# PEER routing decode: candidates laid out in two parts, low ranks compared with 20 of them and high ranks with all 50

## The chip, the cores and the metric

The kernel runs on one core of a Trainium2 chip. The metric is device time in microseconds (us), from the start to the end of one execution. Three runs of the kernel before took 1103.86, 1105.05 and 1106.35 us, median 1105.05. Its parts are TensorE (PE in the profile; PEld is its weight load), VectorE (DVE), ScalarE (ACT), GpSimd (POOL) and SyncE (SP, which issues most DMAs).

## The reference, cut to what matters

One decoder layer over 256 tokens of width 1024: three groups of attention heads with one output projection and a layer norm, then PEER, and a second layer norm. The change lies in PEER. For each token and each of 8 heads:

```python
v1, i1 = lax.top_k(s1, 16)           # of 128 sub-keys, first half
v2, i2 = lax.top_k(s2, 16)           # second half
cand     = v1[..., :, None] + v2[..., None, :]          # 16 x 16
cand_idx = i1[..., :, None] * 128 + i2[..., None, :]
top_s, top_j = lax.top_k(cand, 16)
experts = take_along_axis(cand_idx, top_j)
gate = softmax(top_s)
```

The output is the sum over the 128 (head, rank) slots of gate x gelu(x . u[expert]) x v[expert], with 16384 experts. All is float32.

## The kernel before, in words

**Candidates.** Both lists are sorted, so the pair (i, j) (from 0) can be among the best n only if (i + 1)(j + 1) <= n. For n = 16 these are 50 pairs of 256. `COUNT[i] = 16 // (i + 1)` says how many j a row i has, and rows with equal counts are written together: `RUNS` has 7 entries.

**Tiles.** The 256 tokens are T = 2 tiles of 128, one token in a partition. The expert stage runs over NK = 128 blocks of 128 experts, dense: `expert_in(c)` on TensorE is 24 matmuls for block c (8 pieces of the contraction, three products of split-precision halves), then ScalarE takes the gelu, and `expert_out(c)` multiplies with v. A block needs its u weights split: ScalarE copies the high half (`u_split`, line 948, ring of three), VectorE subtracts it from the weights for the low half (`fill`, line 1319). TensorE waits for that low half before each block.

**Order on VectorE** (in-order; the list is written out by hand). Subkey tops of tile 0 (`subkey_tops`, `top16`, lines 1322 to 1341), `route(0, False)`, `fill(3)`, eight times a pair of subkey tops of tile 1 with one fill, `route(1, True)`, the softmax denominators (lines 1408 to 1415), fills up to N0 - 1, then 64 gate groups, each with a fill. With `mixed` true, `route` and `top16` put a fill behind nearly each step: one after the candidates, three in `top16`, twelve in the comparison. The fills so far are counted at compile time: NROUTE = 27 at the end of `route(1, True)`.

**`route(t, mixed)`** (line 1347). It turns the indices to floats (1348), multiplies the first half's by 128 (1354), adds up values and indices of the candidates for each run (1359), takes the top 16 of the 50 of each head (1364), hands out the shifted values (1365), and then finds the expert number of each rank. That is a comparison with all candidate positions: for two heads at a time an is_equal of 2 x 16 ranks x 50 positions (1373), a multiply by the candidates' expert numbers (1378) and a reduce over the 50 (1382). Four such groups cover the 8 heads, in `eq`, 6400 columns of the arena. Lines 1386 to 1392 split the expert number into block and row, three `tensor_scalar` and one `scalar_tensor_tensor`, each waiting for the one before.

**Around it.** TensorE, in the meantime, computes the queries and subkey scores of tile 1; the last of 32 copies of them is ScalarE's line 960 (`q_saved`). Then come the expert blocks. The transposes of the routes stand ahead of block NTURN = 28, and from block N0 = 32 on each of 64 blocks is preceded by the gate matmuls of four tokens. Blocks below N0 put their gelu into the arena directly; blocks from N0 on go through the buffer `gel`, with a multiply for each on VectorE (1450). The arena columns of those later blocks must be set to one beforehand. GpSimd does most of it:

```python
pool.wait_ge(q_saved, 4 * PH)
pool.wait_ge(x1_split, 4)
nc.gpsimd.memset(arena[:, N0 * S:A_S1], 1.0)                         # 401
nc.gpsimd.memset(arena[:, A_END:A_V], 1.0).then_inc(ones_low, 1)     # 402
```

A third (404) waits for the shifted values of both tiles, and three more (418 to 420) stand behind the first one-hots of the gate stage. A_END is the end of `eq`.

Of the kernel before, what the change touches and what calls it, by code (L numbers as in the profile page):

```python
# [10 lines left out]
ALU = mybir.AluOpType  # L11
ACT = mybir.ActivationFunctionType
AX_X = mybir.AxisListType.X

P = 128
# [12 lines left out]
PH = 8  # L28
NK = 128
TK = 16  # L30
# [3 lines left out]
TAKEN = -3e38  # L34
TWO_PI = (6.28125, 0.0019350051879882812, 2 * np.pi - 6.28125 - 0.0019350051879882812)
PI_IN = 3.1415925
N0 = 32
NROUTE = 27
NTURN = 28
POOL_HOT = 2  # L40
GN = S // 4
UR, UH = 6, 3
# [16 lines left out]
SLOTS = 16  # L59


COUNT = [TK // (i + 1) for i in range(TK)]
OFF = [sum(COUNT[:i]) for i in range(TK)]
NCAND = sum(COUNT)
RUNS = []
for _i in range(TK):
    if RUNS and RUNS[-1][2] == COUNT[_i]:
        RUNS[-1] = (RUNS[-1][0], RUNS[-1][1] + 1, COUNT[_i])
    else:
        RUNS.append((_i, 1, COUNT[_i]))  # L70

K_ID, K_IOTA, K_TRI, K_CB, K_FREQ = 0, 128, 256, 512, 512 + T * NC
# [36 lines left out]
A_EX = A_S1 + 2048  # L111
A_R = A_EX + 1024
A_EQ = A_R + 1472
A_END = A_EQ + PH * TK * NCAND
A_XT0 = A_WMQ
A_V = A_ALL - 1024

# [11 lines left out]
def peer_layer_kernel(nc, x, xT, memT, positions, w_tok, w_memq, w_memk, w_memv, w1k, w1v, w2k, w2v, peT,  # L129
                      w_out, ln1, wq, subk, uT, pv, ln2, consts, out):  # L130
    with ExitStack() as ctx:
# [23 lines left out]
        kc = slab[:, 6144:6144 + K_ALL]  # L155
# [8 lines left out]
        def ar(at, n):  # L164
            return arena[:, at:at + n]

        ident = kc[:, K_ID:K_ID + P]
        iota = kc[:, K_IOTA:K_IOTA + P]


# [36 lines left out]
        h = ar(A_H, T * C_ALL).rearrange("p (t n) -> p t n", t=T)  # L207
# [34 lines left out]
        IF = ar(A_R, 256).rearrange("p (b k) -> p b k", b=2 * PH)  # L242
        cand = ar(A_R + 256, PH * NCAND).rearrange("p (h c) -> p h c", h=PH)
        cande = ar(A_R + 656, PH * NCAND).rearrange("p (h c) -> p h c", h=PH)
        tv = ar(A_R + 1056, 128).rearrange("p (h k) -> p h k", h=PH)
        ti = ar(A_R + 1184, 128).bitcast(U32).rearrange("p (h k) -> p h k", h=PH)
        tf = ar(A_R + 1312, 128).rearrange("p (h k) -> p h k", h=PH)
        gs = ar(A_R + 1440, 16)
        ex = ar(A_EX, 768).rearrange("p (t a s) -> p t a s", t=T, a=3)
        te = ar(A_EX + 768, 256).rearrange("p (t h k) -> p t h k", t=T, h=PH)  # L250
        eq = ar(A_EQ, PH * TK * NCAND)
        assert A_END <= A_WMQ
        G = arena[:, :].rearrange("p (c t) -> p c t", c=NK)
        ln2_sb = ar(0, 2048).rearrange("p (a n) -> p a n", a=2)
# [135 lines left out]
        def _(pool):  # L390
# [9 lines left out]
            pool.wait_ge(x1_split, 4)  # L400
            nc.gpsimd.memset(arena[:, N0 * S:A_S1], 1.0)
            nc.gpsimd.memset(arena[:, A_END:A_V], 1.0).then_inc(ones_low, 1)
            pool.wait_ge(g_shift, 2)
# [15 lines left out]
            nc.gpsimd.memset(arena[:, A_V:A_ALL], 1.0)  # L419
            nc.gpsimd.memset(arena[:, A_R + 4096:A_END], 1.0).then_inc(ones_high, 1)  # L420
            for g in range(2, GN):
# [7 lines left out]
        def _(pe):  # L429
# [317 lines left out]
            def turn_routes():  # L747
                for t in range(T):
                    pe.wait_ge(route_ready, t + 1)
                    for a in range(3):  # L750
                        last = nc.tensor.transpose(ps[:, 2 + t, a * P:(a + 1) * P], ex[:, t, a, :], ident)
                    last.then_inc(pe_rT, 1)

            def gates(g):
                pe.wait_ge(oh_ready, g + 1)
                pe.wait_ge(oh2_ready, g + 1)
                pe.wait_ge(oh3_ready, g + 1)
                if g >= GB:
                    pe.wait_ge(pre_gated, g - GB + 1)
                for q in range(4):  # L760
                    last = mm(ps[:, gate_bank(g), q * P:(q + 1) * P], hot(g)[:, 0, q, :], hot(g)[:, 1, q, :],
                              q == 0, True)
                last.then_inc(pe_g, 1)

            pe.wait_ge(x1_split, 4)
            for c in range(NK):
                if c == NTURN:
                    turn_routes()
                if 0 <= c - N0 < GN:
                    gates(c - N0)  # L770
                expert_in(c)
# [29 lines left out]
        def _(act):  # L801
# [142 lines left out]
            def u_split(c):  # L944
                act.wait_ge(u_in[c % UR], (c // UR + 1) * 16)
                if c >= UH:
                    act.wait_ge(pe_h, c - UH + 1)
                nc.scalar.copy(hi[:, c % UH, :], u_raw(c)).then_inc(u_hi, 1)  # L948
# [17 lines left out]
            def gelu(c):  # L966
                act.wait_ge(pe_h, c + 1)
                if c < N0:
                    nc.scalar.activation(arena[:, c * S:(c + 1) * S], ps[:, c % 2, 0:S], ACT.Gelu).then_inc(gelu_done, 1)
                else:  # L970
                    if c >= N0 + 2:
                        act.wait_ge(gated, c - N0 - 1)
                    nc.scalar.activation(gel[:, c % 2, :], ps[:, c % 2, 0:S], ACT.Gelu).then_inc(gelu_done, 1)  # L973
# [28 lines left out]
            for c in range(NK):  # L1002
                gelu(c)
                if c + UH < NK:
                    u_split(c + UH)
                if c + UH == NROUTE - 1:
                    route_exp()
                if c == NTURN - 1:
                    save_routes()
                    act.wait_ge(rT_saved, T)  # L1010
                    onehot(0)
                    fill_ones(0)
                if c == NTURN:
                    fill_ones(1)
# [21 lines left out]
        def _(dve):  # L1036
            v = nc.vector
            count = [0]

            def did(ins):  # L1040
                count[0] += 1
                ins.then_inc(dve_chain, 1)

            def settle():
                dve.wait_ge(dve_chain, count[0])
# [297 lines left out]
            def spread(mixed, n=1):  # L1343
                if mixed:
                    fill(n)

            def route(t, mixed):
                did(v.tensor_copy(IF, IX[:, t, :, :]))
                settle()
                i1 = IF.rearrange("p (h a) k -> p h a k", a=2)[:, :, 0, :]  # L1350
                i2 = IF.rearrange("p (h a) k -> p h a k", a=2)[:, :, 1, :]
                v1 = V[:, t, :, :].rearrange("p (h a) k -> p h a k", a=2)[:, :, 0, :]
                v2 = V[:, t, :, :].rearrange("p (h a) k -> p h a k", a=2)[:, :, 1, :]
                did(v.tensor_scalar(i1, i1, float(NK), None, ALU.mult))
                settle()
                for r0, r, c in RUNS:
                    sl = slice(OFF[r0], OFF[r0] + r * c)
                    for o, a1, a2 in ((cand, v1, v2), (cande, i1, i2)):
                        did(v.tensor_tensor(o[:, :, sl].rearrange("p h (r c) -> p h r c", r=r),  # L1359
                                            a1[:, :, r0:r0 + r].unsqueeze(3).to_broadcast([P, PH, r, c]),  # L1360
                                            a2[:, :, 0:c].unsqueeze(2).to_broadcast([P, PH, r, c]), ALU.add))
                spread(mixed)
                settle()
                top16([(tv[:, hh, :], ti[:, hh, :], cand[:, hh, :]) for hh in range(PH)], mixed)
                v.tensor_tensor(te[:, t], tv, tv[:, :, 0:1].to_broadcast([P, PH, TK]), ALU.subtract).then_inc(g_shift, 1)

                did(v.tensor_copy(tf, ti))
                settle()
                for h0 in range(0, PH, 2):
                    eqh = eq[:, h0 * TK * NCAND:(h0 + 2) * TK * NCAND].rearrange("p (h k c) -> p h k c", h=2, k=TK)  # L1370
                    eqm = eqh.rearrange("p h k c -> p (h k) c")
                    tfl = tf[:, h0:h0 + 2, :].rearrange("p h k -> p (h k)")
                    did(v.tensor_tensor(eqm, tfl.unsqueeze(2).to_broadcast([P, 2 * TK, NCAND]),  # L1373
                                        kc[:, K_IOTA:K_IOTA + NCAND].unsqueeze(1).to_broadcast([P, 2 * TK, NCAND]),
                                        ALU.is_equal))
                    spread(mixed)
                    settle()
                    did(v.tensor_tensor(eqh, eqh, cande[:, h0:h0 + 2, :].unsqueeze(2).to_broadcast([P, 2, TK, NCAND]),  # L1378
                                        ALU.mult))
                    spread(mixed)  # L1380
                    settle()
                    did(v.tensor_reduce(tfl, eqm, AX_X, ALU.add))  # L1382
                    spread(mixed)
                settle()
                tfl = tf.rearrange("p h k -> p (h k)")
                did(v.tensor_scalar(ex[:, t, 0, :], tfl, 1.0 / NK, -(NK - 1) / (2.0 * NK), ALU.mult, ALU.add))
                settle()
                did(v.tensor_scalar(ex[:, t, 0, :], ex[:, t, 0, :], MAGIC, None, ALU.add))
                settle()
                did(v.tensor_scalar(ex[:, t, 0, :], ex[:, t, 0, :], -MAGIC, None, ALU.add))  # L1390
                settle()
                did(v.scalar_tensor_tensor(out=ex[:, t, 1, :], in0=ex[:, t, 0, :], scalar=-float(NK), in1=tfl,
                                           op0=ALU.mult, op1=ALU.add))
                settle()
# [56 lines left out]

            assert filled[0] == NROUTE
            while filled[0] < N0 - 1:
# [109 lines left out]
```

## Time and profile before

| | us |
|---|---|
| median of 3 runs | 1105.05 |
| profiled execution, device time | 1104.46 |
| its span, first to last instruction | 1102.6 |
| TensorE busy | 1045.7 (95%) |
| VectorE busy | 772.2 (70%) |
| ScalarE busy | 433.0 (39%) |
| GpSimd busy | 109.0 (10%) |
| chain that ended last: TensorE / VectorE | 83% / 14% of the span |
| TensorE waiting for VectorE's low halves (line 1319) | 18.6, the longest 12.0 |

The page divides the span by engine; the chain of waits follows the work back from the last instruction, at each step to what released it. The mean granted TensorE clock was 0.964 of full speed. A stretch in which an engine stands in the chain is one where its work sets the end; its busy share elsewhere says little.

### The profile page before, as it was taken

The numbers are of one execution on the slowest core, as the hardware profiler recorded it, in microseconds if no ns is written. First come the engines' busy times: TensorE is split into PE (matmuls) and PEld (weight loads), VectorE is DVE, ScalarE is ACT, GpSimd is POOL, SyncE is SP. The second block draws the span as 40 slices with busy tenths as digits, with TensorE's granted clock in tenths as the row PEclk, the third lists the DMA queues.
The fourth block names the chain that finished last, engine by engine and source line by source line (L and its number), as shares of the span: only waits on it lengthen the run. The fifth ranks groups of instructions, "written<-read, shape, count | busy, mean of one in ns | idle before, by whom it ended". The sixth has DMA issues, their size and how long they took to land.

```text
span 1102.6 us, 17393 instructions
## 1 busy us (share of the span) xinstructions
PE 1045.7 (95%) x6508; PEld 912.4 (83%) x6508; DVE 772.2 (70%) x1817; ACT 433.0 (39%) x767; POOL 109.0 (10%) x210
## 2 busy tenths in 40 slices
PE   6999889899598999999999999989999999999996
PEld 2458766489588999999999999988888888888885
DVE  1253345368999969999999975556666666666667
ACT  0242233322333464554554544443333333333341
POOL 1000000000300043333333300000000000000000
PEclk9989659999899999999999999999999999999999
DMA  9607100059244554444444445546555555555551
GB/s 336 284 1 286 39 1 0 1 172 341 80 135 143 183 170 138 136 147 140 134 147 142 135 159 185 183 180 239 197 195 191 191 193 192 197 196 195 192 191 38
DMA packets 48610, 176.50 MB, mean 160 GB/s; under 512 B 5120, under 2 KB 6160, under 8 KB 47248
## 3 DMA queue, kind: packets, MB, share of 16 engines
q1 hardware_dynamic: 48128, 173.82, 45.9%
q0 software_dynamic: 400, 1.58, 0.4%
q8 instruction: 52, 0.85, 0.3%
q14 instruction: 30, 0.25, 0.1%
HBM read 174.33 MB, written 1.05 MB: 159 GB/s over the span
## 4 chain that ended last, share of the span: by engine, by line
PE 83%; DVE 14%; DMA 1%; ACT 1%; issue 1%; SPq 0%; DVEq 0%
PE ps L431 81%; DVE lo L1319 2%; DVE arena L1328 1%; DVE arena L1378 1%; DVE arena L1382 1%; DVE arena L1373 1%; DMA arena<-in_w_tok 1%; PE ps L579 1%; DVE arena L1325 1%; DVE arena L1334 1%; DVE hi L1319 0%; DVE ahl L1319 0%; DVE arena L1359 0%; ACT arena L874 0%; PE ps L490 0%
## 5 line engine op out<-in xcount | busy, mean ns | idle before, releaser
L431 PE MATMUL ps<-x1hl,hi 128*128 128x256 f32 x2216 | 380.3, 286 | 18.6 <-DVE lo L1319 17.2
L431 PEld LDWEIGHTS ps<-x1hl,hi 128*128 128x128 f32 x2216 | 328.1, 192 | 20.8 <-issue 12.2
L431 PE MATMUL ps<-hi,ahl 128*128 128x512 f32 x992 | 266.6, 390 | 3.0 <-DVE lo L1473 3.0
L431 PEld LDWEIGHTS ps<-hi,ahl 128*128 128x128 f32 x992 | 186.8, 188 | 42.0 <-issue 3.1
L1024 ACT CAST hi<-slab 128x1024 fp32r<-128x1024 f32 x128 | 134.5, 1053 | 206.9 <-PE ps L431 206.9
L431 PE MATMUL ps<-x1hl,lo 128*128 128x256 f32 x688 | 195.0, 283 | 0.0
L1473 DVE TENSOR_TENSOR lo<-slab,hi 128x1024 fp32r<-128x1024 f32 x128 | 155.9, 1218 | 0.0
L431 PE MATMUL ps<-lo,ahl 128*128 128x512 f32 x496 | 153.3, 390 | 0.0
L431 PEld LDWEIGHTS ps<-x1hl,lo 128*128 128x128 f32 x688 | 132.2, 192 | 0.0
L431 PE MATMUL ps<-arena 128*128 128x128 f32 (+5 forms) x800 | 114.4, 304 | 4.8 <-ACT arena L874 3.6
L431 PEld LDWEIGHTS ps<-arena 128*128 128x128 f32 (+2 forms) x800 | 101.8, 202 | 19.9 <-issue 9.5
L1319 DVE TENSOR_TENSOR lo<-slab,hi 128x1024 fp32r<-128x1024 f32 x86 | 106.0, 1234 | 16.9 <-ACT hi L948 16.6
L431 PE MATMUL ps<-arena,slab 128*128 128x512 f32 (+2 forms) x256 | 105.3, 565 | 10.7 <-DMA arena<-in_w_tok 9.7
L948 ACT CAST hi<-slab 128x1024 fp32r<-128x1024 f32 x107 | 111.2, 1040 | 0.4 <-DMA slab<-in_uT 0.4
L431 PEld LDWEIGHTS ps<-lo,ahl 128*128 128x128 f32 x496 | 93.6, 189 | 19.5
L1485 DVE CAST ahl<-arena 128x256 fp32r<-128x256 f32 x124 | 36.4, 294 | 103.6 <-PE ps L431 103.5
L973 ACT ACTIVATE gel<-ps 128x256 f32<-128x256 f32 x96 | 36.9, 384 | 163.8 <-PE ps L431 163.8
L431 PEld LDWEIGHTS ps<-arena,slab 128*128 128x128 f32 x256 | 48.9, 224 | 53.3 <-issue 39.1
L412 POOL TENSOR_SCALAR slab<-slab,n 128x128 f32<-128x128 f32 x128 | 78.0, 622 | 149.8 <-PE ps L431 149.6
L431 PE MATMUL ps<-slab 128*128 128x128 f32 (+1 forms) x576 | 84.1, 290 | 0.0
L431 PEld LDWEIGHTS ps<-slab 128*128 128x128 f32 x576 | 76.0, 194 | 2.9 <-issue 1.0
L1426 DVE TENSOR_SCALAR slab<-slab 128x128 f32<-128x128 f32 x256 | 75.9, 336 | 0.0
(193 smaller groups left out, 860.2 us busy)
## 6 DMA issues: line engine op xcount, KB each, us to landing
slab<-in_pv SPq DMA_DIRECT2D x128, 512.0 KB, 3.2
slab<-in_uT SPq DMA_DIRECT2D x107, 512.0 KB, 3.3
arena<-in_wq SPq DMA_DIRECT2D x32, 512.0 KB, 4.9
ahl_raw<-in_uT SPq DMA_DIRECT2D x21, 512.0 KB, 3.2
arena<-in_w_tok SPq DMA_DIRECT2D x2, 2048.0 KB, 16.3
arena<-in_w_out SPq DMA_DIRECT2D x1, 4096.0 KB, 12.1
arena<-in_w_tok SPq DMA_DIRECT2D x4, 512.0 KB, 8.1
arena<-in_w_tok SPq DMA_DIRECT2D x1, 1792.0 KB, 19.0
```

What stands on the lines that cost most here:

```text
L412: ins = nc.gpsimd.tensor_scalar(hot(g)[:, 0, q, :], iota, n2[:, g % 2, q:q + 1], None, ALU.is_equal)
L431: return nc.tensor.matmul(o, lhsT, rhs, start=start, stop=stop, skip_group_check=True)
L579: last = nc.tensor.transpose(ps[:, 2, b * P:(b + 1) * P], xb[u % 3][:, b * P:(b + 1) * P], ident)
L948: nc.scalar.copy(hi[:, c % UH, :], u_raw(c)).then_inc(u_hi, 1)
L973: nc.scalar.activation(gel[:, c % 2, :], ps[:, c % 2, 0:S], ACT.Gelu).then_inc(gelu_done, 1)
L1024: nc.scalar.copy(hi[:, c % VH, :], raw[:, v_slot(c), :]).then_inc(v_hi, 1)
L1319: v.tensor_tensor(u_rest_of(c), u_raw(c), hi[:, c % UH, :].bitcast(F32), ALU.subtract).then_inc(u_lo, 1)
L1325: did(v.max(vals[:, o:o + 8], s))
L1328: did(v.max_index(idx[:, o:o + 8], vals[:, o:o + 8], s))
L1426: ins = v.tensor_scalar(hot(g)[:, 1, q, :], iota, slotT[:, 0, tok], slotT[:, 2, tok], ALU.is_equal, ALU.mult)
L1473: v.tensor_tensor(lo[:, v_slot(c), :], raw[:, v_slot(c), :], hi[:, c % VH, :].bitcast(F32), ALU.subtract).then_inc(v_lo, 1)
L1485: v.tensor_copy(o[:, 0, :], a).then_inc(a_hi, 1)
```

## The change

`RUNS` now has two parts. The first holds the 20 pairs with (i + 1)(j + 1) <= 8, in 4 runs; the second the remaining 30, in 7 runs, each run with its columns c0 to c1 of the second list and its place at0. The comparison has three groups in place of four: ranks 0 to 7 of all 8 heads with the first 20 positions (8 x 8 x 20 = 1280 elements an instruction), then ranks 8 to 15 of four heads with all 50 (4 x 8 x 50 = 1600), twice. `eq` shrinks from 6400 to 4480 columns, and A_END moves down with it. There are nine fills in the comparison of the second tile and not twelve, so NROUTE, NTURN and N0 fall by three, to 24, 25 and 29.

```diff
--- before.py
+++ after.py
@@ -34,9 +34,9 @@
 TAKEN = -3e38
 TWO_PI = (6.28125, 0.0019350051879882812, 2 * np.pi - 6.28125 - 0.0019350051879882812)
 PI_IN = 3.1415925
-N0 = 32
-NROUTE = 27
-NTURN = 28
+N0 = 29
+NROUTE = 24
+NTURN = 25
 POOL_HOT = 2
 GN = S // 4
 UR, UH = 6, 3
@@ -59,15 +59,21 @@
 SLOTS = 16
 
 
-COUNT = [TK // (i + 1) for i in range(TK)]
-OFF = [sum(COUNT[:i]) for i in range(TK)]
-NCAND = sum(COUNT)
+HK = TK // 2
 RUNS = []
-for _i in range(TK):
-    if RUNS and RUNS[-1][2] == COUNT[_i]:
-        RUNS[-1] = (RUNS[-1][0], RUNS[-1][1] + 1, COUNT[_i])
-    else:
-        RUNS.append((_i, 1, COUNT[_i]))
+NCAND = 0
+for _low, _high in ((0, HK), (HK, TK)):
+    for _i in range(TK):
+        _c0, _c1 = _low // (_i + 1), _high // (_i + 1)
+        if _c0 == _c1:
+            continue
+        if RUNS and RUNS[-1][0] + RUNS[-1][1] == _i and RUNS[-1][2:4] == (_c0, _c1):
+            RUNS[-1] = (RUNS[-1][0], RUNS[-1][1] + 1, _c0, _c1, RUNS[-1][4])
+        else:
+            RUNS.append((_i, 1, _c0, _c1, NCAND))
+        NCAND += _c1 - _c0
+    if _high == HK:
+        NLEAD = NCAND
 
 
 
@@ -111,7 +117,7 @@
 A_EX = A_S1 + 2048
 A_R = A_EX + 1024
 A_EQ = A_R + 1472
-A_END = A_EQ + PH * TK * NCAND
+A_END = A_EQ + PH * HK * (NLEAD + NCAND)
 A_XT0 = A_WMQ
 A_V = A_ALL - 1024
 
@@ -165,6 +171,7 @@
             return arena[:, at:at + n]
 
         ident = kc[:, K_ID:K_ID + P]
+        codes = kc[:, K_IOTA:K_IOTA + NCAND]
         iota = kc[:, K_IOTA:K_IOTA + P]
 
 
@@ -248,7 +255,7 @@
         gs = ar(A_R + 1440, 16)
         ex = ar(A_EX, 768).rearrange("p (t a s) -> p t a s", t=T, a=3)
         te = ar(A_EX + 768, 256).rearrange("p (t h k) -> p t h k", t=T, h=PH)
-        eq = ar(A_EQ, PH * TK * NCAND)
+        eq = [ar(A_EQ, PH * HK * NLEAD), ar(A_EQ + PH * HK * NLEAD, PH * HK * NCAND)]
         assert A_END <= A_WMQ
         G = arena[:, :].rearrange("p (c t) -> p c t", c=NK)
         ln2_sb = ar(0, 2048).rearrange("p (a n) -> p a n", a=2)
@@ -1353,12 +1360,13 @@
                 v2 = V[:, t, :, :].rearrange("p (h a) k -> p h a k", a=2)[:, :, 1, :]
                 did(v.tensor_scalar(i1, i1, float(NK), None, ALU.mult))
                 settle()
-                for r0, r, c in RUNS:
-                    sl = slice(OFF[r0], OFF[r0] + r * c)
+                for r0, r, c0, c1, at0 in RUNS:
+                    c = c1 - c0
+                    sl = slice(at0, at0 + r * c)
                     for o, a1, a2 in ((cand, v1, v2), (cande, i1, i2)):
                         did(v.tensor_tensor(o[:, :, sl].rearrange("p h (r c) -> p h r c", r=r),
                                             a1[:, :, r0:r0 + r].unsqueeze(3).to_broadcast([P, PH, r, c]),
-                                            a2[:, :, 0:c].unsqueeze(2).to_broadcast([P, PH, r, c]), ALU.add))
+                                            a2[:, :, c0:c1].unsqueeze(2).to_broadcast([P, PH, r, c]), ALU.add))
                 spread(mixed)
                 settle()
                 top16([(tv[:, hh, :], ti[:, hh, :], cand[:, hh, :]) for hh in range(PH)], mixed)
@@ -1366,20 +1374,19 @@
 
                 did(v.tensor_copy(tf, ti))
                 settle()
-                for h0 in range(0, PH, 2):
-                    eqh = eq[:, h0 * TK * NCAND:(h0 + 2) * TK * NCAND].rearrange("p (h k c) -> p h k c", h=2, k=TK)
-                    eqm = eqh.rearrange("p h k c -> p (h k) c")
-                    tfl = tf[:, h0:h0 + 2, :].rearrange("p h k -> p (h k)")
-                    did(v.tensor_tensor(eqm, tfl.unsqueeze(2).to_broadcast([P, 2 * TK, NCAND]),
-                                        kc[:, K_IOTA:K_IOTA + NCAND].unsqueeze(1).to_broadcast([P, 2 * TK, NCAND]),
+                for part, h0, h1 in ((0, 0, PH), (1, 0, PH // 2), (1, PH // 2, PH)):
+                    nh, n = h1 - h0, NCAND if part else NLEAD
+                    eqh = eq[part][:, h0 * HK * n:h1 * HK * n].rearrange("p (h k c) -> p h k c", h=nh, k=HK)
+                    tfp = tf[:, h0:h1, part * HK:(part + 1) * HK]
+                    did(v.tensor_tensor(eqh, tfp.unsqueeze(3).to_broadcast([P, nh, HK, n]),
+                                        codes[:, 0:n].unsqueeze(1).to_broadcast([P, HK, n]).unsqueeze(1).to_broadcast([P, nh, HK, n]),
                                         ALU.is_equal))
                     spread(mixed)
                     settle()
-                    did(v.tensor_tensor(eqh, eqh, cande[:, h0:h0 + 2, :].unsqueeze(2).to_broadcast([P, 2, TK, NCAND]),
-                                        ALU.mult))
+                    did(v.tensor_tensor(eqh, eqh, cande[:, h0:h1, 0:n].unsqueeze(2).to_broadcast([P, nh, HK, n]), ALU.mult))
                     spread(mixed)
                     settle()
-                    did(v.tensor_reduce(tfl, eqm, AX_X, ALU.add))
+                    did(v.tensor_reduce(tfp, eqh, AX_X, ALU.add))
                     spread(mixed)
                 settle()
                 tfl = tf.rearrange("p h k -> p (h k)")
```

## Rows read from the trace of the kernel before

**Rows 1.** Chain of waits in order of time: start us, us, what.
```profile
264.87 1.90 DVE arena L1359 x14
...
295.94 2.95 DVE arena L1386
298.91 2.92 DVE arena L1388
302.44 1.24 DVE lo L1319
303.81 4.35 PE ps L431 x24
...
391.88 3.14 PE ps L431 x24
395.67 344.75 PE ps L431 x2912
```

**Rows 2.** Windows: length, busy us of each engine, TensorE clock, DMA share, GB/s.
```profile
core 0: us, PE busy (x) PEld busy (x) DVE busy (x) ACT busy (x) POOL busy (x), PEclk, DMA share, GB/s
292.00:304.00 12.00, 0.19 (x1) 0.22 (x2) 11.76 (x9) 1.38 (x2) 9.74 (x2) 0.68 0.00 0
...
392.00:742.00 350.00, 348.41 (x2942) 348.20 (x2942) 286.16 (x582) 175.86 (x334) 92.16 (x195) 1.00 0.45 152
```

**Rows 3.** Timeline of VectorE, first decode: start us, us, instruction.
```profile
266.79 0.99 DVE L1325 MAX8 arena<-arena 128x8 f32<-128x50 f32 x8
...
274.02 1.83 DVE L1373 TENSOR_TENSOR arena<-arena,slab 128x1600 f32<-128x1600 f32 x1
275.88 1.83 DVE L1378 TENSOR_TENSOR arena<-arena 128x1600 f32<-128x1600 f32 x1
277.75 1.82 DVE L1382 TENSOR_REDUCE arena<-arena 128x32 f32<-128x1600 f32 x1
279.48 1.82 DVE L1373 TENSOR_TENSOR arena<-arena,slab 128x1600 f32<-128x1600 f32 x1
...
292.23 1.82 DVE L1378 TENSOR_TENSOR arena<-arena 128x1600 f32<-128x1600 f32 x1
...
301.85 0.23 DVE L1390 TENSOR_SCALAR arena<-arena 128x128 f32<-128x128 f32 x1
```

**Rows 4.** Timelines of GpSimd and of ScalarE, 290 to 302 us.
```profile
290.70 0.27 ACT L960 COPY gel<-ps 128x128 f32<-128x128 f32 x1 [1.52 <-PE ps L431]
291.02 7.78 POOL L401 MEMSET arena<- 128x9216 f32 x1 [286.30 <-ACT gel L960]
298.74 3.00 POOL L402 MEMSET arena<- 128x3392 f32 x1
```

**Rows 5.** Groups of instructions by form, line 1359: busy us, mean ns, idle before.
```profile
L1359 DVE TENSOR_TENSOR arena<-arena 128x64 f32<-128x64 f32 x8 | 1.4, 219 | 0.0
L1359 DVE TENSOR_TENSOR arena<-arena 128x24 f32<-128x24 f32 x4 | 0.5, 178 | 0.0
```

**Rows 6.** Timeline of VectorE, from the second tile's first waiting fill on.
```profile
309.61 1.23 DVE L1319 TENSOR_TENSOR lo<-slab,hi 128x1024 fp32r<-128x1024 f32 x1 [0.79 <-ACT hi L948]
...
338.65 1.22 DVE L1319 TENSOR_TENSOR hi<-slab,hi 128x1024 fp32r<-128x1024 f32 x1
...
379.36 1.82 DVE L1373 TENSOR_TENSOR arena<-arena,slab 128x1600 f32<-128x1600 f32 x1
...
387.96 0.23 DVE L1386 TENSOR_SCALAR arena<-arena 128x128 f32<-128x128 f32 x1
...
389.07 0.29 DVE L1410 TENSOR_REDUCE arena<-arena 128x8 f32<-128x128 f32 x1
...
390.60 1.22 DVE L1319 TENSOR_TENSOR lo<-slab,hi 128x1024 fp32r<-128x1024 f32 x1
```

**Rows 7.** Timeline of TensorE: last subkey scores; block 15's first, block 26's last matmul.
```profile
291.33 0.46 PE L431 MATMUL ps<-slab,gel 128*128 128x128 f32 x2 [0.45 <-ACT arena L942]
...
356.56 0.50 PE L431 MATMUL ps<-x1hl,hi 128*128 128x256 f32 x2 [0.20 <-DVE lo L1319]
...
391.09 0.28 PE L431 MATMUL ps<-x1hl,lo 128*128 128x256 f32 x1
```

## The prediction

> **What bounds the kernel now.** I read the chain of waits in order of time first [rows 1]. From 264.87 us on, it lies on VectorE: the whole routing decode of the first token tile (lines 1359 to 1392), then the first `fill` (line 1319) at 302.44, and only then TensorE's first expert block at 303.81. It comes back to TensorE for good with block 27 at 391.88; the stretch from 395.67 holds 344.75 us of matmuls without a break. The windows say the same in sums [rows 2]: from 292 to 304 TensorE works 0.19 us of 12 and its granted clock is 0.68; from 392 to 742 it works 348.41 of 350 us. So a microsecond taken from VectorE between 265 and 391 is worth a microsecond of the kernel until TensorE has nothing more to wait for; afterwards it is worth nothing.
>
> Then VectorE's own timeline [rows 3] against GpSimd's [rows 4]. Two `tensor_scalar` of 128 elements (lines 1386 and 1388) stand in the chain with 2.95 and 2.92 us [rows 1]; line 1390, the same shape, takes 0.23 [rows 3], and in the second tile lines 1386 to 1392 together take 1.11 us (387.96 to 389.07 [rows 6]). The difference is GpSimd: its memset of 9216 columns starts at 291.02 and the next, of 3392, at 298.74 [rows 4]. Line 1386, issued at 295.94, ends at 298.89, just behind the end of the first memset; line 1388, issued into the second, ends at 301.83, just behind that one's end (301.74); line 1390 finds no memset and is quick. The multiply of line 1378 at 292.23, inside the first memset, keeps its 1.82 us [rows 3]: the `tensor_tensor` isn't held. So today's first decode ends with 302.44 - 295.94 = 6.50 us for what is 1.11 us of work: 5.39 us of waiting for GpSimd.
>
> The Trainium skill ("SBUF — State Buffer", Who interferes with whom) has the rule: a copy, cast or tensor_scalar of VectorE in a two-port mode and any GpSimd instruction exclude each other for the whole instruction, whoever starts first goes first, and a two-input tensor_tensor collides only with a GpSimd instruction that reads. The trace agrees on each point, with the numbers above.
>
> **The comparison (lines 1369 to 1383).** Before: four groups of two heads, each an is_equal, a multiply and a reduce over 1600 elements, at pitches 1.86, 1.87 and 1.73 us (274.02, 275.88, 277.75, 279.48 [rows 3]): 5.46 a group. After: one group over 8 x 8 x 20 = 1280 elements and two over 4 x 8 x 50 = 1600. A whole group goes, 5.46, and 320 elements go from three instructions. The price of an element: 1600 elements in 1.83 [rows 3] and 64 in 0.219 [rows 5] give 1.05 ns; 320 are 0.333, three times 1.00. Saved: 6.46 us in the first decode. Bounds: proportional to size (20% of 5.46) would save 6.55; if the shorter rows of 20 cost as much as 1600 did, 5.46. I take 6.46: the rows of line 1359 are shorter still and lie on the same straight line.
>
> **The candidates (line 1359).** 7 runs become 11, so 14 instructions become 22, over the same 800 elements. The 14 take 266.79 - 264.87 = 1.92 us [rows 1, 3], of which 800 x 1.05 = 0.84 are elements; the other 1.08 is 0.077 for each instruction, as they follow without a wait. Eight more: 0.62 us at most by that; adding up the forms (a 24-wide one is busy 0.178 [rows 5], and neighbours overlap by 0.08) gives 0.56. I take 0.6. Bounds: 0.4 and, if nothing overlapped, 8 x 0.178 = 1.4.
>
> The Trainium skill ("VectorE: DVE Perf Modes", The TRN2 errata) speaks against this part: every small instruction pays a fixed latency of about 150 cycles anew. Taken at its word that would be 1.25 us for the eight, and 3.0 for the 14 that take 1.92 here; the busy time of one agrees (0.219 for 64), the pitch doesn't.
>
> **The race that it sets up.** Route 0 gets to line 1386 6.46 - 0.6 = 5.86 us earlier: at 290.08. GpSimd's memset doesn't move: it is released by ScalarE's copy of the last query block, 290.70 plus 0.27 [rows 4], which follows TensorE. With the pitch of the second tile (0.26 each, from 1.11 for the four [rows 6]) the three tensor_scalar start at 290.08, 290.34 and 290.60 and end by 290.85, all before 291.02. Both sides start in step (VectorE waits for the last score copy of tile 0), so this difference is fixed and not drawn anew in each run. The margin is 0.42 us for the last of them. The first fill then starts at 290.08 + 1.11 = 291.19 in place of 302.44: 11.25 us earlier, though only 5.86 of work were removed. TensorE, done with its last queries at 291.33 + 0.46 [rows 7], is ready; by the step of today (302.44 to 303.81) it starts at 292.56.
>
> **Up to route 1.** Eight pairs of subkey tops with a fill each follow at 4.15 us ((338.65 - 309.61) / 7 [rows 6]); TensorE's block takes 2.88 ((391.09 + 0.12 - 356.56) / 12 [rows 7]), so VectorE stays the bound. The fill at 309.61 waited 0.79 for ScalarE's half of block 3, because TensorE had started late; after the change block 0 ends at 295.4, ScalarE's gelu and split (0.38 and 1.04 long) are through by 296.9, and VectorE comes at 297.6: the 0.79 goes. These fills and tops now run beside the memsets; the fills are tensor_tensor, and I take both at nothing.
>
> **Route 1.** From fill 10 at 338.65 to fill 27 at 390.60 there are 51.95 us [rows 6]. Out go the last group with its three fills, 387.96 - 379.36 = 8.60, and 1.00 of elements; in come 0.6: 42.95. It ends with block 24, not 27, and NTURN and N0 move by the same three, so all behind it stands as it did against the blocks, but three blocks, 8.64 us, are left over for TensorE. Net 9.00 - 8.64 = 0.36 gained. The three blocks now come after the gate groups, each with a 0.47 us gate multiply on VectorE, hidden behind 2.88. Is TensorE still the follower? From 292.56, 24 blocks without a wait end at 361.7; VectorE hands over block 24 at 291.19 + (338.65 - 302.44 - 0.79) + 42.95 + 1.28 = 370.8. Yes, by 9 us, though the blocks that VectorE passes quickly in between end at 370.6, so nothing more is to be had.
>
> **The later memsets.** Starting at block 29 the first grows by 768 columns and, with the smaller compare space, the second by 1920; the last of the three later ones shrinks as much. Nobody waits for them if the race is won.
>
> **Sum.** 11.25 + 0.79 + 0.36 = 12.4 us. The profiled execution took 1104.46 us (span 1102.6): 1092.1. The median of the runs is 0.59 above it: 1092.7, and that is the forecast.
>
> **Rivals.**
> (a) Late for the race, the other side of zero. If line 1386 comes after 291.02, that is if less than 4.92 us are saved before it, or line 1388 does (under 5.18), the tensor_scalars are held as now, by longer memsets. At 7.72 us for 9216 columns [rows 4] and 0.82 ns a column (from the two lengths) the first ends at 299.4 and the second at 304.0. Line 1386 ends at 299.5, line 1388 at 304.05, the fill comes 0.63 later as today: 304.7, 2.2 later than now. The 0.79 stays, the 0.36 is gained: 1.9 slower, 1106.9. With only the last two held, 1106.6. For it: a margin of 0.42 on sums of twenty rows, and either upper bound above (5.46 saved, or 1.4 added) is enough. Against: both prices lie on straight lines of this trace. The Trainium skill's fixed latency (the same page and section) would put line 1388 at 290.99 and line 1390 at 291.25: (b), or (a) by a hair.
> (b) Only line 1390 is caught (5.18 to 5.44 saved): it ends at 299.5, the fill starts at 299.9, 2.55 earlier than now, and 2.9 are gained: 1102.1.
> (c) The race is won, but MAX8, FIND_INDEX8 or MATCH_REPLACE8 is held by a memset too. No row shows one beside the other; the profile speaks neither way. The first two such instructions after fill 2 would wait for 299.4 and 304.0, fill 3 would start at 306.8 and not 309.61: 2.8 + 0.36 gained, 1101.9.
> (d) The saved work is hidden anyway, or something of the gate stage is disturbed: within a microsecond or two of 1105. Against it, the chain and 12.0 us of idle TensorE.
>
> **Chances.** Forecast 0.72; (a) 0.14; (b) 0.06; (c) 0.04; (d) 0.04. The forecast's own range is 1090.5 to 1094.5; with (b) and (c) taken in, 1090.5 to 1102.5 holds 0.82. A measurement of this kernel can tell about 0.2%, 2.2 us, from no change: faster 0.83 (forecast, b, c and a little of d), same 0.13 (nearly all of a, part of d), slower 0.04.
>
> **What would show it.** In the profile after: lines 1386 to 1390 (the same three instructions) of tile 0 at about 0.23 us each and before GpSimd's first memset; that memset still at 291.0, about 8.4 long; TensorE's idle time before its first expert block under 1 us in place of 12.0, with the clock never falling there; 22 candidate adds within 2.5 us; three instructions of 1280 elements at 1.49; block 24 at about 370.8 and a continuous TensorE afterwards. If the two tensor_scalar are still 3 us or more long, it is (a) or (b); if a MAX8 of 5 us stands behind fill 2, (c). The forecast is wrong if more than 1 us is missing in the saved 5.86, since the 5.39 behind it then goes as well.

## The result, and the profile after

The changed kernel takes 1093.65 us (median of 4 runs, 1090.82 to 1094.25), the kernel before, timed beside it, 1104.71: ratio 0.9891, 95% interval 0.987 to 0.9911. It is faster by 11.1 us, or 1.1%; the forecast was 12.4 less, 1092.7. The profiled execution took 1090.82 us, with a span of 1088.6.

The chain of waits of the changed kernel (start us, us, what) answers to [rows 1]:

```profile
233.07 25.92 PE ps L438 x232
263.33 2.45 DVE arena L1367 x22
...
289.62 3.50 DVE lo L1326 x3
296.04 1.23 DVE lo L1326
...
340.23 32.19 PE ps L438 x264
373.07 353.39 PE ps L438 x2984
728.17 1.15 DVE lo L1480
729.40 344.61 PE ps L438 x1512
```

Lines stand 7 lower now, or 8 in the candidates and the first two steps of the comparison: 1359 is 1367, 1373 is 1381, 1386 is 1393, 1319 is 1326. The tensor_scalar have left the list of the long pieces, and TensorE holds the chain from 340.23, not from 391.88. VectorE's timeline, for [rows 3]:

```profile
273.04 1.49 DVE L1381 TENSOR_TENSOR arena<-arena,slab 128x1280 f32<-128x1280 f32 x1
...
288.50 0.23 DVE L1393 TENSOR_SCALAR arena<-arena 128x128 f32<-128x128 f32 x1
288.76 0.23 DVE L1395 TENSOR_SCALAR arena<-arena 128x128 f32<-128x128 f32 x1
289.03 0.23 DVE L1397 TENSOR_SCALAR arena<-arena 128x128 f32<-128x128 f32 x1
289.29 0.29 DVE L1399 SCALAR_TENSOR_TENSOR arena<-arena 128x128 f32<-128x128 f32 x1
289.62 3.50 DVE L1326 TENSOR_TENSOR lo<-slab,hi 128x1024 fp32r<-128x1024 f32 x3
293.03 0.48 DVE L1332 MAX8 arena<-arena 128x8 f32<-128x128 f32 x2
```

GpSimd's, for [rows 4]:

```profile
289.48 8.44 POOL L408 MEMSET arena<- 128x9984 f32 x1 [284.78 <-ACT gel L967]
297.85 4.54 POOL L409 MEMSET arena<- 128x5312 f32 x1
```

TensorE's, for [rows 7] (the second line is its first expert block):

```profile
289.80 0.46 PE L438 MATMUL ps<-slab,gel 128*128 128x128 f32 x2 [0.45 <-ACT arena L949]
290.99 0.48 PE L438 MATMUL ps<-x1hl,hi 128*128 128x256 f32 x2 [0.73 <-DVE lo L1326]
```

The same first expert block in the kernel before:

```profile
303.81 0.77 PE L431 MATMUL ps<-x1hl,hi 128*128 128x256 f32 x2 [12.02 <-DVE lo L1319]
```

And the window of the changed kernel, for [rows 2]:

```profile
292.00:304.00 12.00, 12.00 (x102) 12.00 (x101) 11.52 (x50) 5.18 (x8) 10.39 (x2) 1.00 0.46 138
```

Read together: the last tensor_scalar starts 0.45 us before the memset and has ended by 289.26; TensorE waits 0.73 us for its first block where it waited 12.02, and its clock stays at full speed (1.00 against 0.68 [rows 2]).

**Where the gain sits.** Whole times carry the attention part, which shifts from one execution to the next: the 232 matmuls with which the query stage opens began anywhere from 231.0 to 238.2 us in twelve profiles. So I measure from the start of that row to the first matmul of the second expert pass, both in the chain of waits (in `three_parts` the row goes on to 502 matmuls, since TensorE gives the chain up later). Before: 743.37 - 234.60 = 508.77 us. After: 729.40 - 233.07 = 496.33, and 731.65 - 235.34 = 496.31 in a second profile. The stretch is 12.44 us shorter; what follows it took 359.2 us in both.

| stretch, first query block to second pass | us | against |
|---|---|---|
| kernel before | 508.77 | |
| changed kernel | 496.33 and 496.31 | before: -12.4 |
| `before_guard` | 504.48 | before: -4.3 |
| `before_stt` | 504.33 | before: -4.4 |
| `layout_only` | 509.89 | before: +1.1 |
| `delay1` | 496.51 | changed: +0.2 |
| `delay_mid` | 506.90 | changed: +10.6 |
| `delay6` | 511.09 | changed: +14.8 |
| `after_guard_delay6` | 497.55 | changed: +1.2 |
| `n0_back` | 496.27 | changed: -0.1 |
| `three_parts` | 494.49 | changed: -1.8 |

### The profile page after: what moved, and what is told of

Its sections match the earlier page's. It is cut to its first block, busy times and chain, and to the rows that moved or that the text cites. A ratio compares the mean times of both kernels' runs of the same rounds, so it can differ in the third digit from the quotient of the medians.

```text
span 1088.6 us, 17412 instructions
## 1 busy us (share of the span) xinstructions
PE 1042.6 (96%) x6508; PEld 908.9 (83%) x6508; DVE 757.0 (70%) x1830; ACT 432.9 (40%) x767; POOL 109.0 (10%) x210
## 4 chain that ended last, share of the span: by engine, by line
PE 87%; DVE 10%; DMA 1%; ACT 1%; issue 1%; SPq 0%; DVEq 0%
PE ps L438 85%; DVE arena L1335 2%; DMA arena<-in_w_tok 1%; PE ps L586 1%; DVE lo L1326 1%; DVE arena L1332 1%; DVE arena L1341 1%; DVE arena L1386 0%; DVE arena L1389 0%; DVE arena L1381 0%; DVE arena L1367 0%; PE ps L624 0%; PE ps L497 0%; ACT arena L881 0%; DVE xs L1521 0%
## 5 line engine op out<-in xcount | busy, mean ns | idle before, releaser
L438 PE MATMUL ps<-arena,slab 128*128 128x512 f32 (+2 forms) x256 | 103.0, 554 | 11.1 <-DMA arena<-in_w_tok 10.4
L438 PEld LDWEIGHTS ps<-arena,slab 128*128 128x128 f32 x256 | 46.4, 210 | 54.1 <-issue 39.6
## 6 DMA issues: line engine op xcount, KB each, us to landing
arena<-in_w_out SPq DMA_DIRECT2D x1, 4096.0 KB, 12.4
```

The source lines that it names most:

```text
L438: return nc.tensor.matmul(o, lhsT, rhs, start=start, stop=stop, skip_group_check=True)
```

## The experiments

Two theories. Port (the name stands for what the prediction took from the Trainium skill; the runs can show which instruction waits for which, not the port): of the 12.4 us some 5 are not work but waiting, two tensor_scalar held by GpSimd's memset, and the change wins them because it brings these instructions in ahead of the memset. Work: the gain is the VectorE time taken out, and the long tensor_scalar have another cause or are harmless.

### Coming later on purpose: delay1, delay_mid, delay6

```diff
+                if not mixed:
+                    for _ in range(6):
+                        did(v.tensor_tensor(gs, IF[:, 0, :], IF[:, 0, :], ALU.add))
+                        settle()
                 did(v.tensor_scalar(ex[:, t, 0, :], tfl, 1.0 / NK, ...))
```

In `delay6` the loop runs six times as shown, in `delay1` once; the last line is shortened. `delay_mid` has a small reduce and one such add there, outside a loop.

> The changed kernel with one small add (16 wide) chained in front of the three tensor_scalar of the first decode, about 0.24 us. In the profile after, these start 0.98, 0.72 and 0.45 us before GpSimd's first memset. Port theory: all three still get in ahead of it, so only the 0.24 shows: the changed kernel's time + 0.2 us. Work theory (the gain is the VectorE work taken out, the port plays no part): also + 0.2. Both expect no tensor_scalar longer than 0.3 us.

> The same with a small reduce and a small add, about 0.56 us: the third tensor_scalar then starts some 0.1 us after the memset has begun, the first two before it. Port theory: it is held to the end of the first memset, about 8 us long, the first fill comes 8.7 us later than in the changed kernel, TensorE idles again, its clock falls, the fill of block 3 waits for ScalarE again (0.8): + 9.4 us, about 1103. Work theory: + 0.6 us, about 1094.2.

> The same with six small adds, about 1.44 us: all three tensor_scalar come after the start of the memset. Port theory: the first is held to the end of the first memset (8.4 us), the second to the end of the second (4.5 us), the third is free: first fill 13.5 us later than in the changed kernel, + 14.3 us with block 3's wait, about 1108, slower than the kernel before. Work theory: + 1.4 us, about 1095.

Measured: `delay1` 1091.41 us, ratio to the kernel before 0.9871 (0.9856 to 0.9886); `delay_mid` 1101.58, 0.9966 (0.9952 to 0.9979); `delay6` 1106.82, 1.0015 (1.0006 to 1.0025). Timeline of `delay_mid`, VectorE and GpSimd:

```profile
288.39 0.23 DVE L1400 TENSOR_SCALAR arena<-arena 128x128 f32<-128x128 f32 x1
288.58 8.42 POOL L408 MEMSET arena<- 128x9984 f32 x1 [283.88 <-ACT gel L967]
288.65 8.42 DVE L1402 TENSOR_SCALAR arena<-arena 128x128 f32<-128x128 f32 x1
```

The third tensor_scalar starts 0.07 us behind the start of the memset and lasts 8.42 us, to 0.07 us behind its end. And of `delay6`:

```profile
289.32 8.42 POOL L408 MEMSET arena<- 128x9984 f32 x1 [284.62 <-ACT gel L967]
289.60 8.22 DVE L1397 TENSOR_SCALAR arena<-arena 128x128 f32<-128x128 f32 x1
297.67 4.60 POOL L409 MEMSET arena<- 128x5312 f32 x1
297.85 4.50 DVE L1399 TENSOR_SCALAR arena<-arena 128x128 f32<-128x128 f32 x1
302.39 0.23 DVE L1401 TENSOR_SCALAR arena<-arena 128x128 f32<-128x128 f32 x1
```

0.24, 0.56 and 1.44 us of added work cost 0.2, 10.6 and 14.8 us of the stretch. The work theory is out: it has no step in it, and 0.32 us more work (`delay_mid` against `delay1`) cost 10.4. `delay6` is rival (a) of the prediction made real, all three late: forecast there 1.9 us slower than before, here 0.15% (1.7 us) slower, in the stretch 2.3. `delay_mid` is rival (b), forecast 2.9 us faster than before, here 0.34% (3.8 us), in the stretch 1.9. My expectations of 9.4 and 14.3 us on top of the changed kernel were 1.2 and 0.5 too low. The first fill moved as expected (8.72 and 13.53 us later), but fill 3 then waited 1.90 and 1.28 us for ScalarE, where I had put 0.8; the next section says why.

### The other side: the kernel before without the collision

`before_guard`:

```diff
             pool.wait_ge(x1_split, 4)
+            pool.wait_ge(u_lo, 1)
             nc.gpsimd.memset(arena[:, N0 * S:A_S1], 1.0)
```

> The kernel before with one wait more on GpSimd: its first memset starts only after the first fill's low half, that is behind the whole first decode. No work is taken out. Port theory: lines 1386 and 1388 of the first tile fall from 2.9 us to 0.23 each, fill 0 starts 5.4 us earlier, 1104.7 - 5.4 = 1099.3 us. Work theory: no change, 1104.7.

`before_stt`, in the first tile only (shortened; o stands for `ex[:, t, 0, :]`):

```diff
-                did(v.tensor_scalar(ex[:, t, 0, :], tfl, ...))      # and the two behind it
+                for src, k in ((tfl, 1.0 / NK), (o, 1.0), (o, 1.0)):
+                    did(v.scalar_tensor_tensor(out=o, in0=src, scalar=k, in1=src, op0=ALU.mult, op1=ALU.add))
+                    settle()
```

> The kernel before, with the three tensor_scalar of the first tile's decode put as scalar_tensor_tensor (two inputs, both the same column range). They leave out the rounding of the block number, so the output isn't the reference's; the times of all other instructions don't hang on it. GpSimd's memset starts where it did. Form theory (only the one-input form is held): the three take 0.3 us each though the memset runs beside them, fill 0 comes 5.2 us earlier, less up to 1.1 for the low clock lasting longer: 1099 to 1101. Rival (whatever reaches the memset late is held, or the wait is the semaphore chain's): two instructions of about 2.9 us remain and the time is that of the kernel before.

Measured: `before_guard` 1097.19 us, ratio 0.9939 (0.9925 to 0.9952); `before_stt` 1098.93, 0.994 (0.9921 to 0.9959). In `before_stt` the memset stays where it was and the three instructions run beside it:

```profile
291.13 7.78 POOL L401 MEMSET arena<- 128x9216 f32 x1 [286.41 <-ACT gel L960]
...
296.04 0.94 DVE L1395 SCALAR_TENSOR_TENSOR arena<-arena 128x128 f32<-128x128 f32 x3
```

In `before_guard` the memset comes later and the tensor_scalar last 0.23 each. So it is neither the place nor the semaphores but the pair: this form of instruction beside a GpSimd memset. The Trainium skill ("SBUF — State Buffer", Who interferes with whom) says just this of a tensor_scalar in a two-port mode, and all runs here agree. They don't show the mode itself, nor what copies and casts would do.

The first fill comes 5.39 and 5.21 us earlier, as expected, but the stretches give back only 4.3 and 4.4 us. The missing microsecond is TensorE's clock. Fill 3 waits longer for ScalarE than in the kernel before (0.79 [rows 6]); in `before_guard`:

```profile
302.29 1.22 DVE L1320 TENSOR_TENSOR lo<-slab,hi 128x1024 fp32r<-128x1024 f32 x1 [1.90 <-ACT hi L949]
```

ScalarE splits the weights of block 3 behind the gelu of block 0, and block 0 is slower: 5.47 us in the chain of waits against 4.35 [rows 1]. In all six kernels whose fill 3 waits behind a long idle time, the wait is the length of block 0 less 3.56 or 3.57 us: 4.35 and 0.79 (kernel before), 5.47 and 1.90 (`before_guard`, `delay_mid`), 5.14 and 1.57 (`before_stt`), 4.85 and 1.28 (`delay6`), 4.78 and 1.22 (`layout_only`). Windows of `before_guard` (columns as in [rows 2]), idle time, then the first 8.2 us of matmuls:

```profile
288.70:295.30 6.60, 0.04 (x1) 0.00 (x0) 6.36 (x9) 1.55 (x2) 0.00 (x0) 0.68 0.00 0
295.30:299.50 4.20, 4.13 (x19) 4.16 (x20) 4.10 (x14) 0.00 (x0) 4.13 (x1) 0.50 0.00 0
299.50:303.50 4.00, 4.00 (x29) 4.00 (x28) 2.06 (x8) 1.32 (x2) 4.00 (x2) 0.78 0.36 130
```

and of the kernel before, the first 4.2 us:

```profile
303.80:308.00 4.20, 4.19 (x25) 4.20 (x26) 4.10 (x14) 0.00 (x0) 0.00 (x0) 0.67 0.00 0
```

At half clock, 1.2 GHz, 19 matmuls fit in 4.2 us where 25 did at a granted clock of 0.67. This also says what the rest of the gain is. Between `before_guard`, where nothing is held, and the changed kernel lie 504.48 - 496.33 = 8.15 us: 5.90 of work in the first decode, 0.36 in the second, and 1.90 of fill 3's wait, which goes because TensorE no longer idles. My expectation for `before_guard` took the 0.79 as a constant; that for `before_stt`, written after it, allowed the 1.1.

### The same delay with the port free: after_guard_delay6

The diffs of `delay6` and of `before_guard` in one.

> The changed kernel with the six small adds (1.44 us) of before, and GpSimd's memset waiting for the first fill's low half. Port theory: with the memset out of the way the adds cost what they last, 1.4 us, and up to 1.9 more if TensorE's 2.2 us of idle time let its clock fall: 1095 to 1097, against 1106.8 with the same adds and no such wait. Rival (the adds themselves upset something else in the decode): about 1107 again.

Beside it, the changed kernel again:

> The changed kernel, unchanged, as the yardstick of the next three: 1093.6 by its first timing, against 1104.9 of the kernel before, 11 to 12.5 us less.

Measured: 1092.75 us, ratio 0.9883 (0.9862 to 0.9905), beside 1092.03, 0.9881 (0.9863 to 0.99), for the changed kernel. The same six adds that cost 14.8 us cost 1.2 once the memset waits. TensorE was idle for 1.99 us and its clock did not fall, so the extra 1.9 of the expectation did not come. With this one line on GpSimd, the gain no longer hangs on the margin of 0.45 us.

### Parts of the change: layout_only and n0_back

`layout_only` is the kernel before with the changed kernel's `RUNS` and candidate loop, and the old comparison.

> The kernel before with the new order of the candidates (22 adds in place of 14) but the old comparison, four groups over 50. Port theory: in the first decode the 0.56 us more are swallowed, since lines 1386 and 1388 wait for the ends of GpSimd's memsets anyway: fill 0 stays 11.4 us behind the start of the first memset, and only the second tile's 0.56 shows: + 0.6 us. Work theory: + 1.1 us, and fill 0 0.56 later against the memset.

`n0_back`:

```diff
-N0 = 29
+N0 = 32
-NTURN = 25
+NTURN = 28
```

> The changed kernel with N0 and NTURN put back to 32 and 28, while the comparison keeps its nine fills (NROUTE 24): the gate stage begins three blocks later than it could. If TensorE bounds everything behind the decode, as the sum assumed, the stretch from the first query block to the start of the second expert pass is the changed kernel's (496.3 us in two profiles) within 0.5 us, and so is the time. Rival (part of the 12.4 us comes from the earlier gate stage): 1 us or more slower.

Measured: `layout_only` 1104.14 us, 0.9996 (0.9981 to 1.0011); `n0_back` 1094.52, 0.9888 (0.9864 to 0.9911). By its median `n0_back` is 0.9 to 2.5 us slower than the changed kernel (1093.65 and 1092.03), with intervals that overlap. But its profiled run opened the query stage at 238.22, 3 to 5 us later than the changed kernel's two, and from there it has the changed kernel's stretch to 0.06 us: the earlier start of the gate stage is worth nothing. For `layout_only` the times can't tell +0.6 from +1.1; its stretch says 1.1, the number of the work theory, but it is made up otherwise. Its timeline:

```profile
287.63 7.78 POOL L407 MEMSET arena<- 128x9216 f32 x1 [282.93 <-ACT gel L966]
293.10 5.26 DVE L1393 TENSOR_SCALAR arena<-arena 128x128 f32<-128x128 f32 x1
295.35 2.93 POOL L408 MEMSET arena<- 128x3392 f32 x1
298.39 0.23 DVE L1395 TENSOR_SCALAR arena<-arena 128x128 f32<-128x128 f32 x1
299.24 3.50 DVE L1325 TENSOR_TENSOR lo<-slab,hi 128x1024 fp32r<-128x1024 f32 x3
306.83 1.23 DVE L1325 TENSOR_TENSOR lo<-slab,hi 128x1024 fp32r<-128x1024 f32 x1 [1.22 <-ACT hi L954]
```

Here a single tensor_scalar was held through both memsets, to 298.36, and the next ones were free: fill 0 stands 11.61 us behind the memset's start, against 302.44 - 291.02 = 11.42 before. So 0.2 came there, 0.4 from fill 3's wait (1.22 for 0.79), 0.5 from the second tile's adds. The swallowing is shown (0.56 of work cost 0.2 at the first fill), the sum was missed by the clock again.

### A step further: three_parts

The three edits, shortened:

```diff
+PARTS = ((0, 8), (8, 12), (12, 16))             # comparison over 20, 35 and 50 candidates
...
+                    did(v.tensor_tensor(both(A_R + 256 + at0, 400, NCAND, 1), both(A_R + r0, up, ...),
+                                        both(A_R + TK + c0, up, ...), ALU.add))     # values and numbers in one
...
+            pool.wait_ge(u_lo, 1)
```

> A step further: ranks 0 to 7 with 20 candidates, 8 to 11 with 35, 12 to 15 with 50 (4000 elements an operation in place of 4480), values and numbers of a run of candidates added by one instruction over both (18 instructions in place of 22), and the memset behind the first fill. First decode 1.5 us (480 x 3 elements at 1.05 ns) + 0.3 (4 instructions at 0.076) shorter. TensorE can start only when its queries are done, 0.7 us earlier than now, and ScalarE's split of block 3 then comes 0.8 late, so about 1.0 of the 1.8 is kept, and 0.3 to 0.4 in the second tile's candidates; its comparison is hidden behind TensorE. 1.4 us less than the changed kernel, 1092.2. Rival (the 4-dimensional add over two far places costs more than two plain ones): the same as the changed kernel, or up to 1 us slower.

Measured: 1088.77 us, ratio to the kernel before 0.9856 (0.9834 to 0.9878), beside 0.9881 (0.9863 to 0.99) for the changed kernel. The intervals overlap, so by time alone the two aren't told apart; the stretch is 1.8 us shorter, against 1.4 expected. Of its timeline:

```profile
261.29 2.20 DVE L1374 TENSOR_TENSOR arena<-arena 128x128 f32<-128x128 f32 x18
275.21 1.32 DVE L1388 TENSOR_TENSOR arena<-arena,slab 128x1120 f32<-128x1120 f32 x1
292.54 1.23 DVE L1328 TENSOR_TENSOR lo<-slab,hi 128x1024 fp32r<-128x1024 f32 x1 [0.32 <-ACT hi L957]
```

The adds over two places cost no more than plain ones (2.20 for 18, 2.45 for 22), and fill 3 waited 0.32 where I had put 0.8: it comes 1.46 us earlier than in the changed kernel. VectorE gets through the second tile's comparison 1.5 us sooner, and that is not in the gain of 1.8: TensorE holds the chain from block 14 on, as in the changed kernel.

## Why the prediction was right

By its steps, each measured from the first query block (234.60 and 233.07, so that the changed kernel's clock times stand 1.53 us before the forecast's), the changed kernel's instruction against its row of before:

- **Work ahead of the tensor_scalar.** Forecast 5.86 less (6.46 - 0.6). Line 1386's successor: 288.50 - 233.07 = 55.43 against 61.34, 5.91 less. The 1280-element instructions last 1.49, the 22 adds 2.45 (0.56 more than 14, from the first add to the MAX8 behind the last).
- **The race.** Forecast a margin of 0.42 for the last tensor_scalar; it was 0.45, in the second profile 0.45 again and in `n0_back` 0.47, so it isn't drawn anew from run to run. The first fill comes 11.29 us earlier (forecast 11.25). That the waiting of 5.4 us was in the sum at all is what put the forecast at 12.4 and not at 7; `before_guard` and `before_stt` show it as a cause, the delays show its edge to within 0.24 to 0.56 us of added work.
- **Fill 3's wait.** Forecast 0.79 gone; it is gone, but the reason given for it, that TensorE had started late, is not the reason. TensorE starts 1.37 us behind the first fill in both kernels (303.81 - 302.44, 290.99 - 289.62). What differs is block 0: the gelu behind it starts 4.37 us after its first matmul before and 3.14 after the change. The term came out right because the working gave block 0 the 2.88 us of a block at full clock; the prediction expected a clock that never falls there, but didn't tie the 0.79 to it. In kernels whose TensorE idled for 6.6 us or more the wait was 0.79 to 1.90.
- **Route 1.** Forecast 9.00 less on VectorE and 8.64 given back as three blocks: the fill of block 24 stands at 368.00 - 233.07 = 134.93 against 156.00 for block 27 before. Of these 21.07 less, 11.29 and 0.79 are the two items above, 8.99 route 1; 12.44 remain at the second pass, so 8.63 went back.
- **Who bounds after.** Forecast a near tie at block 24, 370.6 for TensorE against 370.8 for VectorE, which is 369.1 against 369.3 on the changed kernel's clock. VectorE handed over block 24 at 369.2, TensorE came to it at 369.3. So the tie fell to TensorE: it holds the chain from block 14 (340.23) on, where the forecast still had it as the follower. This changes the sum by nothing but makes later savings in that comparison worthless, as `three_parts` shows.
- **Rival (c)** is refuted by the trace after: two MAX8 take 0.48 at 293.03, inside the memset, and in the kernel before 0.48 at 305.85, outside it; each FIND_INDEX8 and MATCH_REPLACE8 of 128 columns takes 0.28 or 0.29 in both places. The rule of a fixed latency for each small instruction, which the Trainium skill gives ("VectorE: DVE Perf Modes", The TRN2 errata), isn't borne out for a run of independent ones: 8 more cost 0.56, not 1.25.
- **Two sentences that say too much.** The prediction has the trace agree with the Trainium skill on each point. Its rows show two of them: a tensor_scalar waits for a memset, a tensor_tensor doesn't. And it prices every microsecond taken from VectorE between 265 and 391 at one of the kernel; ahead of a held tensor_scalar that isn't so, as `layout_only` (0.56 for 0.2) and the delays (0.32 for 10.4) show.

The forecast's median was 0.95 us low; the stretch is on it (12.44 for 12.4), with each of its three terms within 0.05. The 0.95 is small beside the shift of the attention part between executions (7 us over twelve profiles). What moves that was not tried.

## What to carry to other kernels

A short VectorE instruction that lasts ten times its usual time, and ends when a GpSimd instruction ends, is waiting and not working, though the profile counts it as busy: find it by its duration against its own form elsewhere, and count that wait when you price work ahead of it. The wait goes in steps, not along a slope: less work ahead of it gains next to nothing until an instruction gets in front, and here 0.3 us more lost 10. Order the two engines with a semaphore rather than by luck; here one wait on GpSimd, which has time to spare, does it.

## What the runs showed of the hardware

How long TensorE's clock stays low after idle time didn't follow the length of that time. After 12.0 us idle the first 4.2 us of matmuls had a granted clock of 0.67 (25 matmuls), after 6.6 us (`before_guard`) 0.50 (19), and the next 4 us still 0.78; after 14.3 us (`delay6`) 0.53 and then 1.00. After 1.99 (`after_guard_delay6`) and 0.73 us (changed kernel) it never fell: 1.00, 35 matmuls in 4.2 us.

A GpSimd instruction can be the one that waits. In the gate stage GpSimd runs its own tensor_scalar, which reads as well as writes, in 64 pairs. In the kernel before 62 pairs take 1.18 to 1.29 us and two take 2.23; these two are the only ones in whose first 0.6 us a tensor_tensor of VectorE from two SBUF inputs (line 1319, 1.22 us long, at 408.72 and 412.49) starts. The changed kernel, `layout_only` and `n0_back` have the same picture, two pairs each. From the kernel before:

```profile
408.18 2.23 POOL L412 TENSOR_SCALAR slab<-slab,n 128x128 f32<-128x128 f32 x2 [2.57 <-PE ps L431]
415.71 1.19 POOL L412 TENSOR_SCALAR slab<-slab,n 128x128 f32<-128x128 f32 x2 [1.39 <-PE ps L431]
```

Beside a memset, which only writes, the same tensor_tensor keeps its time (3.50 us for three, in the changed kernel beside one and in the kernel before without one). No run was made to test this.

A held tensor_scalar sometimes gets in between two memsets that follow each other (kernel before, `delay6`, and just ahead of the second in `delay_mid`) and sometimes not (`layout_only`, held 5.26 us through both); what decides it is open. Where it gets in, the second memset pays a little too: 3.00 us against 2.93 in `layout_only`, and 4.60 in `delay6` and `delay_mid` against 4.54 in the changed kernel.
